# Differential-attention scores as packed single-pass products, with units in the order of heads

## The reference

```
def diff_attend(q, k, v, lam):
    s = jnp.einsum('bhjqd,bhjkd->bhjqk', q, k).astype(jnp.float32) * (DA_HALF ** -0.5)
    p = jax.nn.softmax(s, axis=-1)
    w = p[:, :, 0] - lam * p[:, :, 1]
    return jnp.einsum('bhqk,bhkd->bhqd', w.astype(v.dtype), v)
...
q_l = apply_rope(da_heads(dq), cos, sin)
k_l = apply_rope(da_heads(dk), cos, sin)
k_all = jnp.concatenate([k_l, k_c], axis=3)
v_all = jnp.concatenate([v_l, v_c], axis=2)
```

## Time and profile before

| what | us |
|---|---|
| median of 3 runs | 2370.67 (2369.45 to 2372.53) |
| profiled execution, device time | 2370.8 |
| its span, first to last instruction | 2369.0 |
| PE busy | 2342.1 (99%) |
| DVE busy | 1600.7 (68%) |
| ACT busy | 978.1 (41%) |
| POOL busy | 197.7 (8%) |

### The profile page before, as it was taken

The page is one execution under the profiler, slowest core; times in us unless marked ns, Lnnn a source line. Parts: engine busy times, 40 slices in busy tenths (PEclk is TensorE's granted clock), DMA queues, the critical chain, the costliest instruction groups (busy, mean ns, idle before and its releaser), DMA issues.

```text
span 2369.0 us, 35156 instructions
## 1 busy us (share of the span) xinstructions
PE 2342.1 (99%) x12814; PEld 2014.8 (85%) x12814; DVE 1600.7 (68%) x2635; ACT 978.1 (41%) x1625; POOL 197.7 (8%) x186
## 2 busy tenths in 40 slices
PE   8999999999999999999999999999999999999998
PEld 5888889887887778898888898888898888999997
DVE  6998577456546445569885367887665756668876
ACT  5423224434345334363322254232245346555554
POOL 2111000000000000031111000211100000001220
PEclk9999999999999999999999999999999999999999
DMA  8888464232222322327883337775644433556654
GB/s 275 244 249 241 126 209 143 81 98 72 72 63 80 90 80 65 113 83 238 247 243 120 96 85 231 236 237 179 185 116 116 116 98 107 161 137 198 191 162 140
DMA packets 540054, 356.86 MB, mean 151 GB/s; under 512 B 15206, under 2 KB 490896, under 8 KB 539920
## 3 DMA queue, kind: packets, MB, share of 16 engines
q1 hardware_dynamic: 538472, 354.70, 51.0%
q10 hardware_dynamic: 1448, 0.38, 0.1%
HBM read 337.20 MB, written 17.83 MB: 150 GB/s over the span
## 4 chain that ended last, share of the span: by engine, by line
PE 91%; DVE 3%; ACT 2%; issue 2%; DMA 1%; SPq 1%; POOL 0%; DVEq 0%; ACTq 0%; POOLq 0%
PE ps L1015 25%; PE ps L1017 24%; PE ps L1016 24%; PE ps L1380 2%; PE ps L1314 2%; PE ps L1315 2%; PE ps L1313 2%; PE ps L1028 1%; PE ps L1395 1%; PE ps L1107 1%; PE ps L1109 1%; PE ps L1108 1%; PE ps L1356 1%; PE ps L1412 1%; PE ps L1030 1%
## 5 line engine op out<-in xcount | busy, mean ns | idle before, releaser
L2176 DVE TENSOR_TENSOR w_lo<-raw,w_hi 128x1024 fp32r<-128x1024 f32 (+3 forms) x430 | 496.2, 1155 | 480.0 <-ACT w_hi L1518 475.5
L1518 ACT ACTIVATE w_hi<-raw 128x1024 fp32r<-128x1024 f32 (+3 forms) x430 | 423.3, 985 | 895.6 <-PE ps L1017 714.1
L1015 PE MATMUL ps<-u_hi,w_hi 128*128 128x512 f32 (+2 forms) x2176 | 782.2, 359 | 1.7 <-DVE dav L2776 1.0
L1017 PE MATMUL ps<-u_hi,w_lo 128*128 128x512 f32 (+2 forms) x2176 | 772.6, 355 | 0.0
L1016 PE MATMUL ps<-u_lo,w_hi 128*128 128x512 f32 (+2 forms) x2176 | 772.3, 355 | 0.0
L1015 PEld LDWEIGHTS ps<-u_hi,w_hi 128*128 128x128 f32 x2176 | 410.9, 189 | 60.9 <-DVE dav L2776 1.8
L1017 PEld LDWEIGHTS ps<-u_hi,w_lo 128*128 128x128 f32 x2176 | 410.8, 189 | 58.2
L1016 PEld LDWEIGHTS ps<-u_lo,w_hi 128*128 128x128 f32 x2176 | 411.1, 189 | 55.9
L2592 DVE SCALAR_TENSOR_TENSOR ada_acc<-ada_in_up,cs,ada_acc 128x512 f32<-128x512 f32 x378 | 282.1, 808 | 0.0
L1015 PE MATMUL ps<-g,w_hi 128*128 128x512 f32 (+1 forms) x572 | 206.7, 361 | 0.0
L1017 PE MATMUL ps<-g,w_lo 128*128 128x512 f32 (+1 forms) x572 | 203.8, 356 | 0.0
(11 more groups left out here) (334 smaller groups left out, 3467.6 us busy)
## 6 DMA issues: line engine op xcount, KB each, us to landing
raw<-in_ffn_up SPq DMA_DIRECT2D x150, 512.0 KB, 4.7
raw<-in_w_in SPq DMA_DIRECT2D x132, 512.0 KB, 3.8
ada_in_up<-in_w_ada SPq DMA_DIRECT2D x108, 512.0 KB, 4.5
raw<-in_ffn_down SPq DMA_DIRECT2D x67, 384.0 KB, 3.3
fold_out<-ada_acc SPq DMA_DIRECT2D x32, 512.0 KB, 3.4
fold<-fold_out SPq DMA_DIRECT2D x32, 512.0 KB, 5.5
raw<-in_ffn_down SPq DMA_DIRECT2D x42, 320.0 KB, 3.1
h<-in_ffn_up SPq DMA_DIRECT2D x22, 512.0 KB, 4.5
```

Source lines behind the costliest of these rows:

```text
L1015: pe.matmul(ps[bank][:, cols_of], wh, a_hi, start=a, stop=False)
L1017: m = pe.matmul(ps[bank][:, cols_of], wl, a_hi, start=False, stop=b)
L1518: act.activation(hi, whole, ACT.Copy).then_inc(hi_done, 1)
L2176: dve.tensor_tensor(lo, whole, hi.bitcast(F32), ALU.subtract).then_inc(lo_done, 1)
```

## The change

The scores are computed in packed form. For a head and half j, `ks[:, j, :]` holds the keys' hi part on the half's own 64 partitions and their lo part on the other 64. `qs[:, j, 0, :]` holds the queries' hi part on both halves of the partitions, `qs[:, j, 1, :]` their lo part on both. Two fp32r products over all 128 partitions, added in PSUM, give (q_hi + q_lo)(k_hi + k_lo). There is one `qs` and one `ks` for the head in work, in the place of `ada_acc`, `fold` and a part of `value_bias`. So the units go head by head (tiles within a head), and when the last scores of a head are done, the next head's operands are written: ACT makes four copies for the queries and two for the keys, DVE as many subtractions. Head 0's queries are prepared in the projections, as the step ("queries", 0), its keys behind the last dv. New waits keep the shared places apart. Besides, dv 3 now comes before the last two `ysplit` steps, two quarters of the first block of `ada_products` come earlier, and in the last body of `down` weight splits come ahead of some squares.

```diff
@@ proj_order
-    order += [("dv", 1), ("rope", 3), ("rope", 7), ("ysplit", 4), ("ysplit", 5)]
-    order += [("dv", 2), ("ysplit", 6), ("ysplit", 7), ("dv", 3)]
+    order += [("dv", 1), ("rope", 3), ("rope", 7), ("ysplit", 4), ("ysplit", 5), ("queries", 0)]
+    order += [("dv", 2), ("dv", 3), ("ysplit", 6), ("ysplit", 7)]
@@ attention_units
-    return [(head, t, range(2 if t < 2 else 4)) for t in tiles for head in range(HEADS)], 16 * layer
+    return [(head, t, range(2 if t < 2 else 4)) for head in range(HEADS) for t in tiles], 16 * layer
+def next_head(layer, v):
+    n = units_of_head(layer)
+    return (v + 1) // n if (v + 1) % n == 0 and v + 1 < HEADS * n else None
@@ build
+    qs = at("qs", [P, 2, 2, TOK], F32R, 1152)
+    ks = at("ks", [P, 2, TOK], F32R, 1152 + 8192)
@@ SP, mixer, step ("mq", 3), layer 1
+                        sp.wait_ge(sc_ready, 2 * len(attention_units(layer - 1)[0]))
@@ PE, scores
-            if v < HEADS:
-                pe.wait_ge(rope_done, 8 * layer + 2 * (head + 1))
+            if v % units_of_head(layer) == 0:
+                pe.wait_ge(q_ready, HEADS * layer + head + 1)
+                pe.wait_ge(k_ready, HEADS * layer + head + 1)
...
-                half = slice(j * DA_HALF, (j + 1) * DA_HALF)
-                pe.matmul(ps[SCORE_BANK + j][:, 0:len(keys) * P], dqk[half, head, t * P:(t + 1) * P],
-                          dqk[half, 4 + head, 0:len(keys) * P], start=True, stop=True).then_inc(sc_ready, 1)
+                out, moving = ps[SCORE_BANK + j][:, 0:len(keys) * P], ks[:, j, 0:len(keys) * P]
+                pe.matmul(out, qs[:, j, 0, t * P:(t + 1) * P], moving, start=True, stop=False)
+                pe.matmul(out, qs[:, j, 1, t * P:(t + 1) * P], moving, start=False, stop=True).then_inc(sc_ready, 1)
@@ ACT, down
-            squares(n, (2, 3))
+            squares(n, (2,))
             ahead(base, 2, i, 8, down_kn(2, two))
-            squares(n, (4, 5))
+            squares(n, (3, 4))
             ahead(base, 3, i, 8, down_kn(3, two))
+            squares(n, (5,))
@@ ACT
+        def queries_high(layer, head):
+            t = slice(t0_of(layer), TOK)
+            act.wait_ge(rope_done, 8 * layer + 2 * (head + 1))
+            head_free(act, layer, head)
+            for j, own in enumerate(HALF_ROWS):
+                for rows_of in HALF_ROWS:
+                    m = act.activation(qs[rows_of, j, 0, t], dqk[own, head, t], ACT.Copy)
+            m.then_inc(q_high, 1)
+        def keys_high(layer, head):
+            if head == 0:
+                act.wait_ge(evac_dve, BASES[layer, "proj"][2] + PLANS[layer]["dv", 3][3] + 1)
+            head_free(act, layer, head)
+            for j, own in enumerate(HALF_ROWS):
+                m = act.activation(ks[own, j, :], dqk[own, 4 + head, :], ACT.Copy)
+            m.then_inc(k_high, 1)
@@ ACT, mixer (keys_high(layer, 0) stands ahead of the gate stage)
+                    if step[0] == "scores" and next_head(layer, step[1]):
+                        queries_high(layer, next_head(layer, step[1]))
+                        keys_high(layer, next_head(layer, step[1]))
@@ DVE, up (the same two calls are removed behind the third and fourth split)
+                    if base == 0 and isinstance(i, int) and i == 0 and q == 0:
+                        ada_products(ada_in_up, block, 2)
...
+                    if base == 0 and isinstance(i, int) and i == 0 and q == 1:
+                        ada_products(ada_in_up, block, 3)
@@ DVE, down
-            add_squares(n, (1, 2))
             ahead(base, 2, i, 8, down_kn(2, two))
+            add_squares(n, (1, 2))
@@ DVE (keys_low is alike: ks on the other half's rows = keys - their high part)
+        def queries_low(layer, head):
+            t = slice(t0_of(layer), TOK)
+            dve.wait_ge(rope_done, 8 * layer + 2 * (head + 1))
+            dve.wait_ge(q_high, HEADS * layer + head + 1)
+            for j, own in enumerate(HALF_ROWS):
+                for rows_of in HALF_ROWS:
+                    m = dve.tensor_tensor(qs[rows_of, j, 1, t], dqk[own, head, t], qs[own, j, 0, t].bitcast(F32),
+                                          ALU.subtract)
+            m.then_inc(q_ready, 1)
@@ DVE, mixer (keys_low(layer, 0) stands ahead of the gate stage)
                 elif step[0] == "outputs":
                     outputs(layer, step[1])
+                    if next_head(layer, step[1] + 1):
+                        queries_low(layer, next_head(layer, step[1] + 1))
+                        keys_low(layer, next_head(layer, step[1] + 1))
```

More of the change, by code:

```diff
@@ L245, in attention_units, with units_of_head @@
     tiles = range(2 if layer == DEPTH - 1 else 0, TT)
-    return [(head, t, range(2 if t < 2 else 4)) for t in tiles for head in range(HEADS)], 16 * layer
+    return [(head, t, range(2 if t < 2 else 4)) for head in range(HEADS) for t in tiles], 16 * layer
+def units_of_head(layer):
+    return len(attention_units(layer)[0]) // HEADS
+def next_head(layer, v):
+    n = units_of_head(layer)
+    return (v + 1) // n if (v + 1) % n == 0 and v + 1 < HEADS * n else None
 def gate_order(layer):
@@ L600, in build @@
     ng_split = sem("ng_split")
+    q_high, q_ready, k_high, k_ready = (sem(n) for n in ("q_high", "q_ready", "k_high", "k_ready"))
     ng_ready, s_ready, e_ready, pw_ready = (sem(n) for n in ("ng_ready", "s_ready", "e_ready", "pw_ready"))
@@ L667, in u32_of, with head_free @@
         return u32(n, ITEM_OF[k])[:, k % 2 * SEG:(k % 2 + 1) * SEG]
+    HALF_ROWS = (slice(0, DA_HALF), slice(DA_HALF, P))
+    def head_free(eng, layer, head):
+        if head:
+            units, u0 = attention_units(layer)
+            eng.wait_ge(sc_ready, 2 * (u0 + units_of_head(layer) * head))
+        else:
+            eng.wait_ge(ada_turned, (ADA_OF[1, "up0"] if layer else ADA_OF[0, "up1"]) - 4 +
+                        (ADA_UP + ADA_DOWN[1] if layer else 0))
     def run(eng, count, body, peel_first=False, peel_last=False):
@@ L1970, in mixer @@
                     split_y(y_number(layer, "mo", step[1]), ht[:, step[1], :], yml_hi, step[1], t0)
+                elif step[0] == "queries":
+                    queries_high(layer, 0)
+            keys_high(layer, 0)
             for step in GATE_ORDERS[layer]:
@@ L2510, in body @@
                                           ).then_inc(g_ready, 1)
-                    if base == 0 and isinstance(i, int) and i == 0 and q in (1, 2):
-                        ada_products(ada_in_up, block, q + 1)
                 if add:
@@ L2625, in down @@
             centre(n, (4, 5, 6, 7))
+            ahead(base, 2, i, 8, down_kn(2, two))
             add_squares(n, (1, 2))
-            ahead(base, 2, i, 8, down_kn(2, two))
             if block is not None and i <= ADA_DOWN[layer]:
@@ L2879, in ml_numerator, with keys_low @@
                                      ALU.mult, ALU.add).then_inc(hsum_ready, 1)
+        def queries_low(layer, head):
[7 more added lines that the diff above has]
+            m.then_inc(q_ready, 1)
+        def keys_low(layer, head):
+            dve.wait_ge(k_high, HEADS * layer + head + 1)
+            for j, own in enumerate(HALF_ROWS):
+                m = dve.tensor_tensor(ks[HALF_ROWS[1 - j], j, :], dqk[own, 4 + head, :], ks[own, j, :].bitcast(F32),
+                                      ALU.subtract)
+            m.then_inc(k_ready, 1)
         def maxima(layer, v):
@@ L2990, in mixer @@
                     split_y(y_number(layer, "mo", step[1]), ht[:, step[1], :], yml_hi, yml_lo, step[1], t0)
+                elif step[0] == "queries":
+                    queries_low(layer, 0)
                 elif step[0] == "gates":
@@ L2996, in mixer @@
                     rope(layer, step[1])
+            keys_low(layer, 0)
             for step in GATE_ORDERS[layer]:
```

## The result

The changed kernel takes **2389.06 us** (median of 6 runs, 2384.8 to 2392.21) where the kernel before takes 2371.19 in the same comparison; the ratio is 1.0076, with a 95% interval of 1.0066 to 1.0086. The sign of the forecast is right. Its size is not: 18 us more instead of 9, and the time lies one microsecond outside the range. The profiled execution spans 2387.0 us, 18.0 more than the 2369.0 of before.

The account below looks back on a forecast made before the run. TensorE, busy 99% of the span, was taken as the bound. Waits of 13.7 and 6.6 us, less 7.9 for scores and 3.1 for moves, gave +9.3 on 2370.8: forecast 2380 us, range 2372 to 2388.

Parts of the forecast that it names:

- The scores: Attention scores on PE: packed products save 0.33 us in each of 24 units, 7.9 us off PE.
- Steps of the half-row instructions: Packed copies and subtractions of 512 columns: 0.64 us a step on ACT, 0.70 on DVE, without overlap.
- the second rival: Half-row instructions on ACT and DVE overlap like neighbours of equal rows: waits 12.9 instead of 20.3 us, 2372.7; chance 0.20.
- The waits at the changes of heads: PE waits for the next head's packed operands: 3.6, 4.6, 1.9 us in layer 0, 1.3, 2.3 in layer 1; 13.7 us.
- The projections' ends: PE's new waits before the first gate chunks and layer 1's first scores: 2.9, 1.7 and 2.0 us, sum 6.6.
- layer 1's dav: First values' evacuation in layer 1 at 2006.4 instead of 2004.7, so PE's first gate product 1.7 us late.
- the first scores': Layer 1's first scores: PE arrives at 2009.4, packed keys are ready at 2011.4, a wait of 2.0 us.
- The moves: Changed order in up and down: 1.4 us of fold wait and 1.7 of u_lo waits removed, together 3.1 us off.
- the store leaves about 1.6 us sooner: Up stage, SyncE: earlier modulation products let the store leave sooner, removing PE's whole 1.4 us wait behind the fold.
- The waits for u_lo: PE's four waits for late halves of the last down chunks: all 1.7 us removed.
- The clock: Rival: PE's clock falls during the two longest waits, 1.8 us each, +3.7 us, 2383.8; chance 0.16.
- case 3: PE's clock falls during the two longest waits, costing +3.7 us, 2383.8; chance 0.16.

Follow-up runs that it names:

- the run alone: Only the changes of order in up and down, put into the kernel before: 2367.60 us, 0.9985 of the kernel before.

## Why the prediction was wrong, point by point

- **The scores (-7.9): right.** 0.34 us a unit, -7.7 in PE's busy time.
- **Steps of the half-row instructions (0.64, 0.70, no overlap): right,** and so the second rival is out. ACT's four copies of 512 columns took 2.54 us and the two of keys 1.27; DVE's subtractions 2.77 and 1.39.
- **The waits at the changes of heads (13.7): right.** 3.48, 4.45, 1.72, 1.14 and 2.11 us, together 12.9, for 3.6, 4.6, 1.9, 1.3 and 2.3.
- **The projections' ends (6.6): right but for one.** 2.93 for 2.9; layer 1's dav 2.38, 1.4 more than the 0.96 of before, for 1.7; the first scores' 0.94 for 2.0. The last is smaller because its first gate chunk ran in good part at half clock and PE came 1.1 us later; in the kernels with this wait left empty and that chunk at full speed the wait was 1.91 to 2.09.
- **The moves (-3.1): inside the interval of the run alone (1.4 to 5.7), wrong in one of two parts.** The step that failed is "the store leaves about 1.6 us sooner: I take the whole 1.4". It left sooner and landed later, behind two loads of 512 KB issued just ahead of it. The waits for u_lo gave 1.5 of the 1.7.
- **The clock: this is the step that failed.** The forecast put it aside as a rival with a chance of 0.16, priced at 3.7 us: two stretches, behind "the two longest waits". It came behind waits of 2.1 us and more, five times, one of the stretches twice as long, and cost 9.3 us of busy time. With the waits as measured (12.9 + 5.3 - 1.5), the scores (-7.7) and the clock (+9.3) the sum is 18.3; the profile has 18.0. Without the clock it is 9.0, close to the forecast's 9.3 in part by luck: the waits came out 2.1 us shorter and the moves gave 1.6 us less. The rows of before said no more than that 1.4 us of idle time is harmless; the text took the gap between 1.4 and 4.6 as if only its upper end were in doubt, and did not ask what the 2.9, 2.6 and 2.3 us of its own sum would do. Had case 3 been priced for every wait above 1.4 us, it would have stood at six or seven stretches of 1.8 us, some 12 us, and the range would have reached past 2390.

## What to carry to other kernels

On an engine that is busy 99% of the time, an added wait has two prices: its length, and the clock behind it. Price the second one for every new wait that is longer than any in the trace of before, not for the longest alone; here it doubled the loss. (Waits up to 1.8 us did without it; from 1.9 us on it came behind some and not behind others.) And work that is added to ACT and DVE may cost next to nothing or 28 us with the same instructions (2361.20 against 2389.06), by where it stands in their queues: put what can start early in the stretch in which the engine waits for another, and behind the step that PE needs next.

## What the runs showed of the hardware that was not expected

- The granted clock fell behind idle times of TensorE of 2.11 us (at 2069.28) and once of 1.92, but not behind 1.72 (882.25), nor behind 1.91 in two kernels at the same place, nor in the 5 us behind one of 2.19 and one of 2.38. The stretches at half clock are 3.4 or 6.8 us, and the same wait of 3.48 us had one of 6.8 in one kernel and of 3.4 in another. With products whose results nobody reads in the long waits, 66 in all, it did not fall.
- A store of 512 KB on SyncE's queue landed in 3.0 us when nothing was issued just ahead of it, in 3.9 with two loads of 512 KB issued 2.2 us or more before, and in 6.5 with the same two issued 0.6 to 1.0 us before (6.1 and 6.2 at this place in two other kernels).
- ACT's packed copies, which change their rows from one to the next, start only after the one before: 0.64 us a step for 64 rows by 512 columns, where two `yml_hi` splits of 128 rows by 512 columns, on the same rows, start 0.54 apart. DVE's packed subtractions go the same way, 0.70 a step.
